# Two edits in a fused two-block kernel: expert routing, and the mLSTM's second gate by seven products

## The reference, cut to what matters

```python
# first block: which experts a token goes to
gl = (xn @ w_group) + b_group;   grp = argmax(gl)
el = (xn @ w_router) + b_router, the 8 experts of group grp
top_l, top_i = top_k(el, 2)
wgt = p_grp * softmax(top_l)
# each expert: silu(x w1) * (x w3), then w2; rows are added back with wgt

# second block, mLSTM branch: h are the heads' outputs, o and z columns of one projection
h = rms_norm_2(h, head_norm)
return h * sigmoid(o) * silu(z)
```

## Time and profile before

| | |
|---|---|
| median of 3 runs | 1741.76 us (1738.57 to 1742.91) |
| the profiled execution | 1738.36 us |
| its span, first to last instruction | 1735.2 us |
| PE busy | 1686.4 us (97%) |
| DVE, ACT, POOL busy | 854.8, 380.5, 210.8 us |
| chain that ended last | PE 91%, DVE 3%, DMA 3% |
| moved by DMA | 308.61 MB |

### The profile page before, as it was taken

The page is one execution under the profiler, slowest core; times in us unless marked ns, Lnnn a source line. Parts: engine busy times, 40 slices in busy tenths (PEclk is TensorE's granted clock), DMA queues, the critical chain, the costliest instruction groups (busy, mean ns, idle before and its releaser), DMA issues.

```text
span 1735.2 us, 19720 instructions
## 1 busy us (share of the span) xinstructions
PE 1686.4 (97%) x7592; PEld 984.2 (57%) x7592; DVE 854.8 (49%) x1486; ACT 380.5 (22%) x681; POOL 210.8 (12%) x280
## 2 busy tenths in 40 slices
PE   7999999999899999999999999999999999999999
PEld 3887876775433333333334447567865554577664
DVE  3755742454523232323325345766755654686663
ACT  1112210001000000000003102231144433454530
POOL 1233410001000000000001000000224430000000
PEclk9999999999899999999999999999999999999999
DMA  7313122234699999999995022312320021121201
GB/s 286 115 61 122 49 71 87 103 146 191 252 408 427 426 427 426 427 426 428 423 427 213 32 81 111 99 55 100 127 98 1 1 73 49 69 78 49 98 1 48
DMA packets 27872, 308.61 MB, mean 178 GB/s; under 512 B 4415, under 2 KB 4703, under 8 KB 10368
## 3 DMA queue, kind: packets, MB, share of 16 engines
q1 hardware_dynamic: 21312, 289.21, 41.1%
q0 software_dynamic: 6464, 18.10, 3.0%
HBM read 306.57 MB, written 4.19 MB: 179 GB/s over the span
## 4 chain that ended last, share of the span: by engine, by line
PE 91%; DVE 3%; DMA 3%; issue 1%; POOL 1%; ACT 0%; SPq 0%; DVEq 0%; ACTq 0%
PE ps L410 87%; PE ps L413 4%; DMA arena<-in_w 2%; DVE arena L1168 1%; DMA arena<-in_rows 1%; DVE arena L1179 1%; DMA wring<-in_dense 0%; DVE arena L1264 0%; POOL small L2726 0%; ACT arena L2295 0%; DVE small L1183 0%; DVE HT L1195 0%; DVE arena L1195 0%; DVE H L1168 0%; DVE wring L1168 0%
## 5 line engine op out<-in xcount | busy, mean ns | idle before, releaser
L410 PE MATMUL ps<-arena 128*64 128x512 f32 (+13 forms) x2384 | 516.9, 398 | 4.4 <-ACT arena L2295 2.1
L410 PE MATMUL ps<-wring,arena 128*64 128x512 f32 (+2 forms) x1136 | 396.4, 579 | 2.5 <-ACT arena L2295 1.6
L410 PE MATMUL ps<-wring,HT 128*128 128x512 f32 (+1 forms) x1040 | 364.7, 503 | 5.2 <-ACT HT L2295 1.9
L1168 DVE TENSOR_TENSOR arena<-ps,arena 128x512 f32<-128x512 f32 (+1 forms) x197 | 134.8, 684 | 463.6 <-PE ps L410 306.0
L410 PEld LDWEIGHTS ps<-arena 128*64 128x64 f32 (+4 forms) x2384 | 232.7, 154 | 222.9 <-issue 211.2
L410 PEld LDWEIGHTS ps<-wring,HT 128*128 128x128 f32 x1040 | 194.8, 192 | 145.0 <-issue 128.9
L2295 ACT ACTIVATE arena<-ps 128x512 f32<-128x512 f32 (+4 forms) x161 | 86.5, 537 | 609.4 <-PE ps L413 306.3
L410 PEld LDWEIGHTS ps<-wring,arena 128*64 128x64 f32 (+1 forms) x1136 | 147.9, 154 | 122.1 <-issue 118.7
L410 PE MATMUL ps<-HT,wring 128*128 128x512 f32 (+2 forms) x528 | 192.7, 530 | 0.0
L410 PE MATMUL ps<-wring 128*128 128x256 f32 x816 | 185.2, 381 | 0.0
L1168 DVE TENSOR_TENSOR H<-ps,H 128x512 f32<-128x512 f32 x182 | 125.8, 691 | 99.0 <-PE ps L410 90.2
(11 more groups left out here) (109 smaller groups left out, 963.8 us busy)
## 6 DMA issues: line engine op xcount, KB each, us to landing
wring<-in_w SPq DMA_DIRECT2D x48, 2048.0 KB, 20.6
wring<-in_dense SPq DMA_DIRECT2D x39, 2048.0 KB, 8.4
arena<-in_w SPq DMA_DIRECT2D x36, 2048.0 KB, 18.1
HT<-in_w SPq DMA_DIRECT2D x12, 2048.0 KB, 17.5
arena<-in_rows POOLq DMA_DIRECT2D x33, 256.0 KB, 5.0
H<-in_x SPq DMA_DIRECT2D x4, 512.0 KB, 3.8
arena<-in_relb POOLq DMA_DIRECT2D x8, 256.0 KB, 8.1
n_scratch<-arena POOLq DMA_DIRECT2D x4, 512.0 KB, 3.3
```

Source lines behind the costliest of these rows:

```text
L410: return nc.tensor.matmul(o, l, r, start=start, stop=stop, skip_group_check=True)
L1168: done(nc.vector.tensor_tensor(o, a, b, op), tell)
```

## The change

**Routing.** `normed_rows(3)` moves from before the last `routed` to behind the one-hot rows `first` (its function moves out of `stage_a`, and `stage_a` returns the gain rows). TensorE waits for "nb" tile by tile. The running sums `cc` go; `cs5` holds `cs` and 32 zeros, and the counts come from one product with `ustr` over all 160 columns and four with `ones` over 32, 64, 96 and 128 shifted columns, into the same bank. The subtraction for the group softmax stands behind `cs`. ScalarE copies the first half of ("xT", 0) without waiting for the second, and TensorE waits for the first half before w1 and for the second at w1's fifth step. The wait for "keep1" moves to just before `ys` is written.

**m_z.** It becomes seven products, between m_o and n_q. Its result with bias goes to `mz` (on the place of kc), its sigmoid to `sq_z`. VectorE's norm of y1 is spread between its sums; og times mz stands behind them, og times the sigmoid behind n_q's second sum, y1 times og behind n_q's third.

```diff
-          "m_q": (1, None), "m_o": (0, "n_q"), "n_q": (0, "n_kv"), ...
+          "m_q": (1, None), "m_o": (0, "m_z"), "m_z": (0, "n_q"), "n_q": (0, "n_kv"), ...
...
             def stage_b():
                 f = fill("count")
                 pe.wait_ge(S("cc"), saw("cc"))
-                mm(f.ap[:, 0:160], C("ones"), cc.rearrange("p a n -> p (a n)"), stop=False)
-                mm(f.ap[:, 0:128], C("ustr"), cs.rearrange("p a n -> p (a n)"), start=False).then_inc(f.full, 1)
+                csf = cs5.rearrange("p a n -> p (a n)")
+                mm(f.ap[:, 0:160], C("ustr"), csf, True, False)
+                for d in range(4, 0, -1):
+                    ins = mm(f.ap[:, 32 * d:160], C("ones"), csf[:, 0:160 - 32 * d], False, d == 1)
+                ins.then_inc(f.full, 1)
...
-                pe.wait_ge(S("nb"), saw("nb", 4))
                 for a in range(4):
+                    pe.wait_ge(S("nb"), saw("nb"))
...
                 for g in range(NE // 2):
-                    evacuated(("xT", g, 0), ("xT", g, 1))
+                    evacuated(("xT", g, 0))
                     for name in ("w1", "w3"):
...
                         for k in range(8):
+                            if k == 4 and name == "w1":
+                                evacuated(("xT", g, 1))
...
-                w = weight("m_z")
-                for i in range(4):
-                    used["m_z"] = tok(("mz", i), w, i)
-                for p in range(14):
-                    seventh("n_q", p)
+                for key in ("m_z", "n_q"):
+                    for p in range(14):
+                        seventh(key, p)
...
                 heard("inv")
-                normed_rows(3)
                 routed(3)
...
+                memset(cs5[:, 4, :], 0.0)
                 first_max(gl, 4, gm, ohg, mi)
-                tt(ge, gl, bc(gm, 4), SUB, "ge")
...
-                memset(cc[:, 0, :], 0.0)
-                tt(cs, oh1, oh2, ADD)
-                for i in range(4):
-                    tt(cc[:, i + 1, :], cc[:, i, :], cs[:, i, :], ADD, "cc" if i == 3 else "v")
+                tt(cs, oh1, oh2, ADD, "cc")
+                tt(ge, gl, bc(gm, 4), SUB, "ge")
...
                     stt(first[:, a, :], iota[:, 0:128], p8[:, 4 + a:5 + a], first[:, a, :], ALU.is_equal, ADD, "first")
+                normed_rows(3, g_ffn)
                 heard("gx")
...
-                rs = head_norm(y1, qcf, 4, 128)
                 yv = y1.rearrange("p (x d) -> p x d", d=128)
-                tt(yv, yv, rs.unsqueeze(2).to_broadcast([128, 16, 128]), MUL)
-                r = row("hn0")
-                tt(y14, y14, r[1].unsqueeze(1).to_broadcast([128, 4, 512]), MUL)
+                rg, r = row("hn0"), row("b_mz")
+                for n in range(7):
+                    seventh("m_z", n, behind(mz4), by_row(r))
+                    if n == 0:
+                        heard("hsq")
+                        red(small[:, 8:24], qcf.rearrange("p (x d) -> p x d", d=128), ADD, tell="hss")
+                    elif n == 1:
+                        heard("inv")
+                        tt(yv, yv, small[:, 48:64].unsqueeze(2).to_broadcast([128, 16, 128]), MUL)
+                    elif n == 2:
+                        tt(y14, y14, rg[1].unsqueeze(1).to_broadcast([128, 4, 512]), MUL)
+                        row_done(rg)
                 row_done(r)
-                r = row("b_mz")
                 heard("og")
-                for i in range(4):
-                    a = es[1]
-                    f = full("mz", i)
-                    tt(a, f.ap, r[1], ADD, f)
-                    tt(og4[:, i, :], og4[:, i, :], a, MUL)
-                    heard("me")
-                    tt(og4[:, i, :], og4[:, i, :], es[0], MUL)
-                row_done(r)
-                tt(y1, y1, og, MUL, "y1")
+                tt(og, og, mz, MUL)
...
+                        if n == 1:
+                            heard("me")
+                            tt(og, og, sq_z, MUL)
+                        elif n == 2:
+                            tt(y1, y1, og, MUL, "y1")
...
                 f = full("xT", 0, 0)
-                for i in range(2):
-                    a.wait_ge(S(f"keep{i}"), 32)
-                full("xT", 0, 1)
+                a.wait_ge(S("keep0"), 32)
                 copy(xsT[0][:, 0:4, :], f.ap.rearrange("p (k t) -> p k t", k=4), f)
```

More of the change, by code:

```diff
@@ L102 @@
           "w_ga0": (0, "w_ga1"), "w_ga1": (0, "w_gc0"), "w_gc0": (0, "w_gc1"), "w_gc1": (0, "w_o0"), "w_o0": (0, None),
-          "m_q": (1, None), "m_o": (0, "n_q"), "n_q": (0, "n_kv"), "n_kv": (0, "n_z"), "n_z": (1, None), "o_y1": (0, None), "o_y2": (0, None), "o_y3": (0, None)}
+          "m_q": (1, None), "m_o": (0, "m_z"), "m_z": (0, "n_q"), "n_q": (0, "n_kv"), "n_kv": (0, "n_z"), "n_z": (1, None), "o_y1": (0, None), "o_y2": (0, None), "o_y3": (0, None)}
 SEVEN_O = (("a", "A11", "B11"), ("d", "A12", "B21"), ("b", "S2", "T2"), ("c", "S1", "T1"), ("b", "S3", "T3"),
@@ L235, in build @@
         ohg, ge = ar(16, 4), ar(16, 4)
-        elm, cs = (ar(128, 4) for _ in range(2))
+        elm, cs5 = ar(128, 4), ar(160, 5)
+        cs = cs5[:, 0:4, :]
         oh12 = ar(256).rearrange("p (n a e) -> p n a e", n=2, a=4)
         oh1, oh2 = oh12[:, 0], oh12[:, 1]
-        cc = ar(160, 5)
         pos, qq, cnt = ar(128), ar(128), ar(32)
@@ L302, in build @@
         kcd = ar(62)
+        mz, sq_z = sq, nqT.rearrange("p a n -> p (a n)")
+        mz4 = mz.rearrange("p (a n) -> p a n", a=4)
         sums, rcp, causal = ar(64), ar(64), nbs[1][:, 0:512]
@@ L1226, in turned @@
                 copy(HT[:, 4:8, i * 128:i * 128 + 128], f.ap.rearrange("p (k t) -> p k t", k=4), f)
-            def head_norm(x, sq, nh, hd):
-                w = 4 * nh
-                ss, r = small[:, 8:8 + w], small[:, 48:48 + w]
-                heard("hsq")
-                red(ss, sq.rearrange("p (x d) -> p x d", d=hd), ADD, tell="hss")
-                heard("inv")
-                return r
             def rope(x4, cos, sin, a, nh, tmp, tell="v"):
@@ L1342, in probs, with normed_rows @@
                 copy(to[x % 4][:, 0:n], f.ap[:, 0:n], f)
+            def normed_rows(i, g):
+                for h in range(2):
+                    o = nbB[i].rearrange("t (k p) -> t k p", k=8)[:, :, 64 * h:64 * h + 64]
+                    x, w = (x.rearrange("t (p k) -> t k p", k=8) for x in (H[:, i, 512 * h:512 * h + 512], g[h][1]))
+                    stt(o, x, small[:, 4 + i:5 + i], w, MUL, MUL, "nb" if h else "v")
+                    if i == 3:
+                        row_done(g[h])
             def stage_a():
@@ L1517, in routed @@
                     stt(logits[:, i, :], f.ap[:, 0:36], small[:, 4 + i:5 + i], misc[1][:, 416:452], MUL, ADD, f)
-                def normed_rows(i):
-                    for h in range(2):
-                        o = nbB[i].rearrange("t (k p) -> t k p", k=8)[:, :, 64 * h:64 * h + 64]
-                        x, w = (x.rearrange("t (p k) -> t k p", k=8) for x in (H[:, i, 512 * h:512 * h + 512], g[h][1]))
-                        stt(o, x, small[:, 4 + i:5 + i], w, MUL, MUL, "nb" if h else "v")
-                        if i == 3:
-                            row_done(g[h])
                 v.wait_ge(S("wr"), 16)
@@ L1531, in stage_a @@
                 heard("inv")
-                normed_rows(0)
+                normed_rows(0, g)
                 turned("B", 0)
@@ L1535, in stage_a @@
                 heard("inv")
-                normed_rows(1)
+                normed_rows(1, g)
                 turned("B", 1)
@@ L1540, in stage_a @@
                 heard("inv")
-                normed_rows(2)
+                normed_rows(2, g)
                 routed(1)
@@ L1546, in stage_a, with stage_b @@
                 heard("inv")
-                normed_rows(3)
                 routed(3)
                 row_done(misc)
-            def stage_b():
+                return g
+            def stage_b(g_ffn):
                 L = logits
@@ L2266, in stage_e @@
                         part(i, h, 6)
-            stage_a()
-            stage_b()
+            stage_b(stage_a())
             stage_c()
@@ L2425, in stage_b @@
                     f = full("y", g, 1)
+                    if not g:
+                        a.wait_ge(S("keep1"), 32)
                     copy(ys[g % 2][:, 512:1024], f.ap, f)
@@ L2522, in stage_d @@
                 squares(y1, qcf, 128)
-                for i in range(4):
-                    freed(("mz", i))
-                    act(es[0], es[1], ACT.Sigmoid, "me")
+                freed(("m_z", "c"))
+                act(sq_z, mz, ACT.Sigmoid, "me")
                 heard("y1")
```

3 lines of the change are left out of this document (2 added, 1 removed).

## The result

The changed kernel takes 1733.47 us (median of 7 runs, 1732.11 to 1734.39). The kernel before, run beside it, takes 1738.57 us (7 runs, 1735.36 to 1742.91). The ratio is 0.997, with a 95% interval of 0.996 to 0.9979: 5.2 us faster, between 3.6 and 6.9.

The account below looks back on a forecast made before the run. TensorE, busy 97% of the span, was taken as the bound, with the weight stream second. Routing -2.5 and m_z/n_q -1.5 sum to -4.0 us: 1734.4 from the profiled execution, 1737.8 on the median; range 1733.5 to 1742.5.

Parts of the forecast that it names:

- rival B: VectorE keeps up in n_q, or the clock rises early in routing: -5.8 us, 1736.0; chance 0.20.
- the two places: Routing up to the first expert product, predicted -2.5 us; m_z then n_q, predicted -1.5 us.
- VectorE to the counts: Routing: shorter VectorE chain lets the counts start at 437.31 instead of 438.83, 1.52 us earlier.
- counting products: Routing on TensorE: five short products instead of two cost +1.36 us, bounds +0.64 to +1.40.
- zeros and narrow products, by the clock: Routing on TensorE: clock rises near 443.3, 6.0 us after resumption; the narrow products end at 450.4 against 451.38.
- first w1 product without a stop: Start of the experts: copying group 0's rows by halves removes TensorE's stop before w1, gain 1.5 us.
- wait for the tables: End of group 0's w1: TensorE newly waits 0.3 us for the row lists' tables, 1.2 if the clock is early.
- end of the experts: Weight stream, released by w1's end, starts and ends 2.5 us earlier; the tables' wait comes out of slack.
- The m_z part: m_z and n_q: -3.3 us by seven products, +0.15 and +1.65 waits before their sixth products, net -1.5.
- (C): First place hidden: weight stream ends when it did, TensorE's 1.5 us wait becomes 4.0; 1740.3; chance 0.13.
- (D): m_z: POOL's root blocks VectorE's two weight sums, a wait of 2.3 us; in all -1.7, 1740.1; chance 0.04.
- (E): Routing: clock stays at 1.2 GHz through the 64 narrow records, making the kernel slower, 1744.4; chance 0.05.

Follow-up runs that it names:

- experiment 1: Changed kernel, but route() again waits for both halves of the transposed tile before its first product; 1735.53 us, ratio 0.9983 to the kernel before.
- experiment 6: Changed kernel with three 2048-wide VectorE operations (the gate products) one place later; 1731.28 us, ratio 0.9965 to the kernel before.
- experiment 3: Kernel before with only m_z made by seven products, routing unchanged; 1736.08 us, ratio 0.9993 to the kernel before.

## Why the prediction was right or wrong

**The step that failed is the one from the sum to the time.** "It lies 3.4 below the median of the runs, 1741.76; on the median the forecast is 1737.8." Those three runs lay high: beside the changed kernel the kernel before took 1738.57 (7 runs, these three among them), later 1737.39 (29 runs), 1737.82 (16) and 1738.56 (17). The profiled execution, 1738.36, was the better base, and from it the same sum gave 1734.4, 0.9 above what was measured. The sum itself, -4.0 us, lies in both measured intervals (3.6 to 6.9 and 2.6 to 5.7 faster). The range names the spread of single runs only for its high end; its low end, 1733.5, lay 1.6 us below rival B with an early clock (1736.0 - 0.9), on the same high base, and it missed by 0.03 us. The wrong base is 3.2 of the 4.3 us between forecast and measurement.

The rest, 1.2 us, has a second step behind it: "span 1735.2 and 3.2 around it" was carried over unchanged, and in the changed kernel 1.8 stand around the span. Inside the span the two places gave 2.45 + 1.06 = 3.5 us in the pair of traces, 0.5 less than the sum, and about 1.0 came outside it, which the prediction put at nothing. That -4.0 fits the measured times is in part luck.

**A term that is missing.** The diff also lets the router products start when ScalarE's half of HT is there. The prediction doesn't name it, and takes the last router products as ending where they did. They moved by 1.40 us (54.18 against 55.58), and experiment 1 shows that undoing this alone puts them back.

**The routing terms**, each from the mark, in the pair of traces:

| term | predicted | measured |
|---|---|---|
| router products by halves | not there | -1.40 |
| VectorE to the counts | -1.52 | -1.48 |
| counting products | +1.36 (0.64 to 1.40) | +1.28 |
| zeros and narrow products, by the clock | -0.8 | -1.55 |
| first w1 product without a stop | -1.5 | -1.56 |
| first w1 product, sum | -2.5 (1.7 to 3.4) | -4.71 |
| wait for the tables | +0.3 (to 1.2) | +1.35 |
| end of the experts | -2.5 | -2.45 |

Term by term: the VectorE chain was read well. The counts took 434.86 to 437.23, where the first of the zeros starts: 2.37 us, inside the bounds, and the same within 0.01 in all eleven traces with five counting products. By columns alone they would have taken 1.73 (0.64 more than before); the four products of 32 to 128 columns took 0.43 each on average, what the one of 128 columns took before, and the row on 36 columns had said so. The clock rose 4.3 us after TensorE resumed, and the prediction took 6.0 from its one example; over the twelve other traces it came 4.0 to 5.5 us after, so the example was the latest of all. So 0.74 of the -1.55 are the zeros (2.67 us instead of 3.41), the rest the narrow products.

**Where the early start went.** The forecast gave the experts' end to the stream of weights, and the stream to w1's end. That is the step of the mechanism that failed: the first expert product came 4.71 us earlier, the load that w1's end releases was issued 4.71 earlier too, and the experts ended 2.45 earlier. What was lost between them was lost by TensorE. 1.35 went to the wait for the tables, which delays w3, and about 0.9 between the transposes and the experts' end: from those transposes to group 1's first product it took 1.05 longer (the branch), from there to the HT load 0.38 longer (the clock), and 0.55 came back between the load and the end, 0.45 of it because the one wait for a weight load was shorter (1.05 instead of 1.50). That the sum came out at -2.5 was luck, two errors that met: 2.2 us more at the first expert product than forecast, and as much lost behind it.

**The m_z part.** Predicted -3.3 + 0.15 + 1.65 = -1.5, measured -3.3 + 0.59 + 1.65 = -1.06. The wait in n_q is right to the hundredth, with its place and its cause, and experiment 6 shows the cause by removing it. The one in m_z is the mis-sized term: VectorE's fourth sum was to end 17.11 us after m_z's start and ended at 1172.07, 17.63, since it stood idle for 0.47 us ahead of it. In experiment 3 the fourth sum ends just as late (17.62), and there the same 0.47 stands ahead of the multiplication by the root and is put down to POOL:

```profile
1163.49 2.29 DVE L1183 TENSOR_REDUCE small<-arena 128x16 f32<-128x2048 f32 x1
...
1169.57 2.29 DVE L1168 TENSOR_TENSOR arena<-arena,small 128x2048 f32<-128x2048 f32 x1 [0.47 <-POOL small L2729]
```

The root's answer came 3.79 us behind the reduction there, not 3.42. In the changed kernel's own trace the idle time sits elsewhere, and what it waited for isn't settled.

**The rivals.** (B) "VectorE keeps up in n_q": refuted by the row at 1198.04; its other half, the early clock, came (rise before 440). (C) Refuted: the wait for a weight load didn't grow, it fell from 1.5 to 1.0. The 2.3 us by which the gain shrank, 4.71 to 2.45, went to the tables' wait, the branch and the clock, and none of it to the stream. (D) Refuted by the two sums of 1.23 under the root. By the Trainium skill, "SBUF — State Buffer", on the shared port pair, the weight sums should have waited until 1165.5; in this kernel's rows they don't. (E) Refuted, the clock rose early.

## What to carry to other kernels

A forecast in absolute time is no better than its base: before adding a sum to the median of three runs, compare it with the profiled execution, and put the base's own spread on both ends of the range. Go through the diff once more for waits that were only split or moved, since a wait for half of a result moves everything behind it. Compare the spans as well as the times: here about 1.0 us of the difference lay outside them. Where a stream of loads at full share follows, look first whether TensorE stops at all in it; if it doesn't, what an early start is worth is decided by TensorE's own stops before that stretch (here the tables, the branch, the clock). A distance that is constant in every trace doesn't name the load at its start as the cause, since the load is issued at a fixed point of TensorE's work. Large elementwise operations that share a queue with sums TensorE waits for belong one to a turn: moving three of them by one place was worth 2.2 us.

## What the runs showed that I had not expected

- The stop behind group 0, where TensorE reads a number and branches, lasted 3.46 to 5.50 us in thirteen traces of nearly the same program, and half of an earlier arrival seems to be lost in it: 3.66 to 3.88 in the three that arrive latest (103.6 to 104.6), 5.26 to 5.33 in three of the four that arrive first (100.0 to 100.3). But 3.84, 4.14 and 3.46 occur too, and five traces that arrive within 0.02 us of each other (101.24 to 101.26) have 3.46, 4.77, 4.96, 5.35 and 5.50, so the scatter is as large as the trend. What it waits for no row shows. It stays open.
- TensorE and the stream of weights are balanced almost to nothing: over some 180 MB (an estimate, 425 us at 425 GB/s) the stream holds TensorE up once, for 0.80 to 1.50 us, and from group 1's first w1 to the end of the experts it is 424.80 to 425.61 us in thirteen traces of ten kernels.
- The time at which the granted clock falls after TensorE has stopped, or nearly, varies from one execution to the next: in experiments 1 and 3 it fell while the last router products ran, in the other traces between their end and 3.6 us behind it. In experiment 1 that cost 0.94 us.
